# Layer 1 of an expert layer by lookup: 768 columns of V read densely instead of gathered

## What the reference computes

```python
for i in range(DEPTH):                       # DEPTH = 2, 256 tokens, D_MODEL = 2048
    h = rms_norm(x, norm_mix_g[i])
    y = mla_mixer(h, ...) if i % 2 == 0 else fox_mixer(h, ...)
    x = x + y
    h = rms_norm(x, norm_ffn_g[i])
    x = x + peer_ffn(h, peer_w_q[i], peer_sub_keys[i], peer_u[i], peer_v[i])

def peer_ffn(h, w_q, sub_keys, u, v):        # 8 heads, 128 keys a side, 16384 experts, top 16
    q = (x @ w_q).reshape(t, PEER_HEADS, 2, PEER_D_HALF)
    scores = jnp.einsum('thcd,cnd->thcn', q, sub_keys)
    top_s, top_i = lax.top_k(scores, PEER_TOPK)
    cand_s = top_s[..., 0, :, None] + top_s[..., 1, None, :]
    cand_i = top_i[..., 0, :, None] * PEER_N_KEYS + top_i[..., 1, None, :]
    best_s, pos = lax.top_k(cand_s.reshape(...), PEER_TOPK)
    idx = jnp.take_along_axis(cand_i.reshape(...), pos, axis=-1)
    g = jax.nn.softmax(best_s, axis=-1)
    # for each block of 128 tokens, n_sel = 8 heads x 16 = 128 experts a token
    u_sel = u[i_blk]
    a = gelu(einsum('tkd,td->tk', u_sel, x_blk), approximate=False) * g_blk
    return einsum('tk,tkd->td', a, v[i_blk])
```

## Time and profile before

| what | us |
|---|---|
| median of 3 runs | 3615.15 (3604.41 to 3617.04) |
| the profiled execution | 3612.59 |
| its span in the profile | 3610.6 |
| TensorE busy | 2886.4 |
| VectorE busy | 2035.0 |
| GpSimd busy | 1465.2 |
| ScalarE busy | 945.4 |
| data moved by DMA | 1345.35 MB |

### The profile page before, as it was taken

One profiled execution on the slowest core, in us unless ns is written; L12 is line 12 of the kernel. 1 busy time (PEld: TensorE's weight loads), 2 busy tenths in 40 slices (PEclk: granted clock), 3 DMA queues, 4 the chain that ended last, 5 costly groups with the idle time before them and its releaser, 6 DMA issues.

```text
span 3610.6 us, 26702 instructions
## 1 busy us (share of the span) xinstructions
PE 2886.4 (80%) x7322; PEld 1357.2 (38%) x7322; DVE 2035.0 (56%) x3584; ACT 945.4 (26%) x2349; POOL 1465.2 (41%) x1065
## 2 busy tenths in 40 slices
PE   7888977777777888888888788998988777777776
PEld 6445743333332433333333343443433322222222
DVE  2333166666667554555464655455546466677765
ACT  3334322222222222323221222232322122222221
POOL 4002545555565322222342532222244355555554
PEclk8877989899998999999998899999999898888888
DMA  4212589999999999999999999999999999999998
GB/s 147 79 61 89 177 358 416 416 416 416 415 410 422 418 417 418 417 417 414 412 396 399 418 418 417 417 417 417 413 411 399 399 371 421 421 422 421 421 419 351
DMA packets 262853, 1345.35 MB, mean 373 GB/s; under 512 B 27200, under 2 KB 48192, under 8 KB 130368
## 3 DMA queue, kind: packets, MB, share of 16 engines
q0 software_dynamic: 147456, 1073.81, 72.0%
q1 hardware_dynamic: 115264, 269.99, 19.9%
HBM read 1341.62 MB, written 2.10 MB: 372 GB/s over the span
## 4 chain that ended last, share of the span: by engine, by line
DMA 60%; PE 20%; issue 12%; POOL 3%; DVE 3%; ACT 1%; SPq 1%; DVEq 0%; POOLq 0%; ACTq 0%
DMA room<-in_peer_v_dram,index 50%; PE psum L977 11%; DMA wbuf<-in_fox_w_o_dram 5%; PE psum L1026 3%; DMA wbuf<-in_peer_w_q_dram 3%; DMA room<-in_peer_u_dram,index 2%; POOL room L668 1%; PE psum L1041 1%; PE psum L740 1%; PE psum L741 1%; PE psum L742 1%; POOL room L678 1%; DVE resid L1974 0%; SPq L536 0%; POOL w_low L652 0%
## 5 line engine op out<-in xcount | busy, mean ns | idle before, releaser
L977 PE MATMUL psum<-room,diag 128*128 128x512 f32 x3072 | 1612.9, 667 | 565.4 <-DMA room<-in_peer_v_dram,index 517.6
L1963 DVE CUSTOM_DVE_ANT_0 room<-room,normed 128x2048 f32<-128x2048 f32 x512 | 1172.7, 2290 | 619.7 <-DMA room<-in_peer_u_dram,index 615.8
L678 POOL DMA_INDIRECT room<-in_peer_v_dram,index x512 | 757.3, 1479 | 1096.8 <-PE psum L977 1040.4
L977 PEld LDWEIGHTS psum<-room,diag 128*128 128x128 f32 x3072 | 605.2, 208 | 1510.5 <-issue 1257.7
L668 POOL DMA_INDIRECT room<-in_peer_u_dram,index x512 | 591.6, 1155 | 719.2 <-DVE dots L1963 468.7
L1392 ACT ACTIVATE acts<-dots 128x1 f32<-128x1 f32 x512 | 103.4, 202 | 1779.6 <-DVE dots L1963 1779.1
L1974 DVE SCALAR_TENSOR_TENSOR resid<-room,acts,resid 128x512 f32<-128x512 f32 x512 | 384.6, 751 | 308.1 <-DMA room<-in_peer_v_dram,index 239.7
L1041 PE MATMUL psum<-wbuf,normedT 128*128 128x512 f32 x1024 | 464.0, 596 | 0.0
L1026 PE MATMUL psum<-wbuf,normedT 128*128 128x512 f32 x512 | 273.5, 684 | 78.5 <-DMA wbuf<-in_fox_w_o_dram 40.7
L1041 PEld LDWEIGHTS psum<-wbuf,normedT 128*128 128x128 f32 x1024 | 189.2, 190 | 215.5 <-issue 212.9
L652 POOL TENSOR_TENSOR w_low<-wbuf,w_high 128x2048 fp32r<-128x2048 f32 (+1 forms) x28 | 114.0, 4081 | 306.0 <-ACT w_high L1247 306.0
(11 more groups left out here) (199 smaller groups left out, 1794.2 us busy)
## 6 DMA issues: line engine op xcount, KB each, us to landing
wbuf<-in_fox_w_in_dram SPq DMA_DIRECT2D x128, 1024.0 KB, 12.6
wbuf<-in_fox_w_o_dram SPq DMA_DIRECT2D x32, 1024.0 KB, 31.8
wbuf<-in_peer_w_q_dram SPq DMA_DIRECT2D x32, 1024.0 KB, 28.1
wbuf<-in_mla_w_o_dram SPq DMA_DIRECT2D x16, 1024.0 KB, 5.2
wbuf<-in_peer_w_q_dram SPq DMA_DIRECT2D x32, 512.0 KB, 20.1
wbuf<-in_mla_w_in_dram SPq DMA_DIRECT2D x8, 1024.0 KB, 8.2
wbuf<-in_mla_w_kvb_dram SPq DMA_DIRECT2D x32, 256.0 KB, 3.4
room<-in_peer_u_dram,index POOLq DMA_INDIRECT x512, 17.0
```

The source lines that it names most:

```text
L678: pool.indirect_dma_start(v_ring[:, r, :], None, v_table, bass.IndirectOffsetOnAxis(index[:, number % 2, s:s + 1], 0)).then_inc(v_full[r], 16)
L977: mm = pe.matmul(psum[:, q, :], diag[:, r, :], v_ring[:, r, q * TILE:(q + 1) * TILE], start=at == 0, stop=at == WINDOW - 1, skip_group_che ...
L1963: V.tensor_tensor_reduce(u_ring[:, r, :], u_ring[:, r, :], normed[:, b, :], 1.0, 0.0, ALU.mult, ALU.add, dots[:, r:r + 1]).then_inc(dot_do ...
```

## The change

Layers and windows 0 and 1 stay as they are. In layer 1 the 256 full V gathers go away, and so do `accumulate` and `axpy` for windows 2 and 3. Columns 768 to 2047 are still gathered (`gather_part`, rows of 5 KB). Of these 256 gathers, 88 are issued in window 3 and summed by TensorE with diagonal matrices that ScalarE builds; the other 168 come after the last dot and are added by VectorE, one operation each (`add_part`). GpSimd issues them all, on the queue of the U gathers.

Columns 0 to 767 are not gathered. SP reads all 16384 rows of V's layer 1 once, as 128 tiles of 128 rows with 3 KB of each row, into four buffers (`load_dense`). The rows of tile i are the experts whose first key is i; its partitions are the second key. TensorE multiplies each tile with a matrix of second key by token, for each of the two token blocks, and sums all 128 tiles in PSUM (`dense`). These spread matrices have to be built first. The keys and the weights of a block are transposed, so that slots lie on partitions; for each token, VectorE builds a one-hot of the second key and a one-hot of the first key times the weight (`one_hots`, four tokens a call: one comparison over 128x512 and four operations over 128x128), TensorE multiplies the two (`spread_tokens`), and ScalarE copies the product into the spread matrix with a stride of 128 elements (`copy_spread`). Block 0 has its 32 calls in window 3; block 1 has its 32 calls after the last dot. The spread matrix of block 0 takes the place of the weight buffer, that of block 1 the whole of `room`, where the U ring was.

```diff
+DENSE = 768
+KEPT = D - DENSE
+GATHERED = 2 * WINDOW
+SPLIT = 2 * WINDOW
+LAST = 3 * WINDOW
+ON_PE = 88
+TOKENS = 4
+BUILDS = P // TOKENS
+BUILD_AT = 8
+def v_at(m):
+    return 3 + m * 124 // ON_PE
+def build_at(g):
+    return BUILD_AT + g * 7 // 2
...
+        spread = [a.rearrange("p (i t) -> p i t", i=KEYS) for a in (wbuf[:, :, :, :].rearrange("p h k n -> p (h k n)"),
+                                                                   room[:, :])]
...
+        v_part = [old_T[:, r * KEPT:(r + 1) * KEPT] for r in range(3)] + [scores_ahead[:, 0:KEPT]]
+        v_tile = [normed[:, 1, 0:DENSE], normed[:, 1, DENSE:2 * DENSE], scores[:, 0:DENSE], scores[:, DENSE:2 * DENSE]]
...
+            def load_dense(i):
+                r = i % RING
+                if i == 0:
+                    sp.wait_ge(dot_done, UNITS * SLOTS)
+                    sp.wait_ge(index_ready, UNITS)
+                if i >= RING:
+                    sp.wait_ge(tile_used, i - RING + 1)
+                sp.dma_start(v_tile[r], peer_v[1][i * KEYS:(i + 1) * KEYS, 0:DENSE]).then_inc(tile_full[r], 16)
...
+            def gather_part(m):
+                b, at, r = m // WINDOW, m % WINDOW, m % RING
+                if m == 0:
+                    pool.wait_ge(late_ready, 1)
+                    pool.wait_ge(score_done, 8)
+                if at % SLOTS == 0 and b:
+                    pool.wait_ge(index_ready, 3 * PHEADS + at // SLOTS + 1)
+                if RING <= m < ON_PE + RING:
+                    pool.wait_ge(part_summed, m - RING + 1)
+                if m >= ON_PE + RING:
+                    pool.wait_ge(part_added, m - RING - ON_PE + 1)
+                pool.indirect_dma_start(v_part[r], None, v_table,
+                                        bass.IndirectOffsetOnAxis(late_place[b][:, at:at + 1], 0),
+                                        element_offset=DENSE).then_inc(part_full[r], 16)
...
-                gather_v(n)
+                if n < SPLIT:
+                    gather_v(n)
...
+                for m in range(ON_PE):
+                    if n == LAST + v_at(m):
+                        gather_part(m)
...
+            for m in range(ON_PE, GATHERED):
+                gather_part(m)
...
+            def sum_part(m):
+                r = m % RING
+                if m == 0:
+                    pe.wait_ge(peer_added, 2)
+                pe.wait_ge(diag2_ready, m + 1)
+                pe.wait_ge(part_full[r], 16 * (m // RING + 1))
+                for c0 in range(0, KEPT, TILE):
+                    n = min(TILE, KEPT - c0)
+                    mm = pe.matmul(psum[:, c0 // TILE, 0:n], diag[:, r, :], v_part[r][:, c0:c0 + n],
+                                   start=m == 0, stop=m == ON_PE - 1, skip_group_check=True)
+                mm.then_inc(part_summed, 1)
...
+            def spread_tokens(b, g):
+                number = BUILDS * b + g
+                bank = 6 + g % 2
+                pe.wait_ge(hot_ready, number + 1)
+                if number > 1:
+                    pe.wait_ge(spread_done, number - 1)
+                for t in range(TOKENS):
+                    last = pe.matmul(psum[:, bank, t * P:(t + 1) * P], hot_key[g % 2][:, t, :], hot_act[g % 2][:, t, :],
+                                     start=True, stop=True)
+                last.then_inc(spread_full, 1)
+            def dense(i):
+                r = i % RING
+                pe.wait_ge(tile_full[r], 16 * (i // RING + 1))
+                if i == 0:
+                    pe.wait_ge(spread_done, NB * BUILDS)
+                    pe.wait_ge(sums_closed, 1)
+                for b in range(NB):
+                    for c0, n, bank in ((0, TILE, 3 + 2 * b), (TILE, DENSE - TILE, 4 - 2 * b)):
+                        mm = pe.matmul(psum[:, bank, 0:n], spread[b][:, i, :], v_tile[r][:, c0:c0 + n],
+                                       start=i == 0, stop=i == KEYS - 1, skip_group_check=True)
+                mm.then_inc(tile_used, 1)
...
-                    accumulate(n)
+                    if window < 2:
+                        accumulate(n)
+                    if window == 3:
+                        last_window(at)
...
+                for at in range(WINDOW, WINDOW + 4):
+                    last_window(at)
+                turn_tables(1)
+                for g in range(BUILDS):
+                    spread_tokens(1, g)
+                for i in range(KEYS):
+                    dense(i)
...
+                    nc.scalar.activation(act_of[n // WINDOW - 2][:, at:at + 1], acts[:, 0, r:r + 1], ACT.Copy,
+                                         scale=gates[:, number % 2, s:s + 1]).then_inc(diag_ready, 1)
+                    return
...
+            def copy_spread(b, g):
+                act.wait_ge(spread_full, BUILDS * b + g + 1)
+                dst = spread[b][:, :, TOKENS * g:TOKENS * (g + 1)].rearrange("p i t -> p t i")
+                nc.scalar.activation(dst, psum[:, 6 + g % 2, :].rearrange("p (t i) -> p t i", t=TOKENS),
+                                     ACT.Copy).then_inc(spread_done, 1)
...
+            def one_hots(b, g):
+                number = BUILDS * b + g
+                if g == 0:
+                    dve.wait_ge(turned_done, b + 1)
+                    dve.wait_ge(iota_ready, 2)
+                if number > 1:
+                    dve.wait_ge(spread_full, number - 1)
+                tokens = slice(TOKENS * g, TOKENS * (g + 1))
+                step(V.tensor_tensor(hot_key[g % 2], iota_key[1].unsqueeze(1).broadcast_to([P, TOKENS, KEYS]),
+                                     turned[b][:, 1, tokens].unsqueeze(2).broadcast_to([P, TOKENS, KEYS]), ALU.is_equal))
+                for t in range(TOKENS):
+                    at = TOKENS * g + t
+                    last = V.tensor_scalar(hot_act[g % 2][:, t, :], iota_key[0], turned[b][:, 0, at:at + 1],
+                                           turned[b][:, 2, at:at + 1], ALU.is_equal, ALU.mult)
+                    if t < TOKENS - 1:
+                        step(last)
+                chain.settle()
+                last.then_inc(hot_ready, 1)
...
+            def add_part(m):
+                b, at, r = m // WINDOW, m % WINDOW, m % RING
+                dve.wait_ge(part_full[r], 16 * (m // RING + 1))
+                dve.wait_ge(part_added, m - ON_PE)
+                if b and at == 0:
+                    dve.wait_ge(diag_ready, UNITS * SLOTS)
+                cols = resid[:, b, DENSE:D]
+                V.scalar_tensor_tensor(out=cols, in0=v_part[r], scalar=late_act[b][:, at:at + 1], in1=cols,
+                                       op0=ALU.mult, op1=ALU.add).then_inc(part_added, 1)
...
-                    if n:
+                    if 0 < n <= SPLIT:
                         axpy(n - 1)
-                    if at == 0 and n:
+                    if n in (WINDOW, SPLIT):
...
+                close_parts()
+                for g in range(BUILDS):
+                    one_hots(1, g)
+                    if g % 2:
+                        add_part(ON_PE + g // 2)
+                for m in range(ON_PE + BUILDS // 2, GATHERED):
+                    add_part(m)
+                for b in range(NB):
+                    add_dense(b)
```

151 lines of the change are left out of this document (139 added, 12 removed).

## The result

| | before | after |
|---|---|---|
| median | 3613.76 us (8 runs, 3604.41 to 3617.04) | 3628.01 us (8 runs, 3624.61 to 3639.84) |
| ratio | | 1.0046 [1.0037, 1.0055] |
| profiled execution, its span | 3612.59, 3610.6 us | 3628.41, 3626.7 us |

The changed kernel is 0.46% slower. The difference is real (the interval leaves out 1), but lies inside the 0.5% that the forecast called no change. The forecast was 3600 us, some 15 us less than before; measured were 14 us more. It was 28 us too low: 3628.01 us lies 3 us above its own range of 3578 to 3625, though inside the wider 3545 to 3650.

What follows compares the result with a forecast made beforehand. DMA traffic was taken to bound the kernel. The stages summed as 2062 + 606 + 466 + 8 + 75 + 369 + 8 = 3594 us of span, given as 3600 us; own range 3578 to 3625, over all cases 3545 to 3650.

Steps and rivals of the forecast that it cites:

- What is removed: Layer 1's V traffic: 637 us of gathers become 530 us of part gathers and dense tiles, at most 107 us less.
- bridge: Between the last dot's window and block 1's builds: last activation, sum, transposes, copy and closing addition, about 8 us.
- Window 2: Layer 1, block 0, with block 1's attention beside it: from 898 to 606 us, bounds 579 and 650.
- slower rival: Layer 1, block 0: attention handshakes set the pace, 645 us there and 3639 us in all; decides from 640; chance 0.24.
- Window 3: Layer 1, block 1: from 644 to 466 us, 458 of transfers plus 8 lost; bounds 458 and 490.
- The signs named for this stage: Layer 1, block 1, in the profile after: about 3.6 us a slot at over 410 GB/s.
- Builds: Block 1's 32 spread-matrix calls after the last dot: 75 us, VectorE at 1.5 us a call plus 16 part additions.
- the full-gain rival: Whole layer 1: all gained but for the builds (1.25 us a call, 66 us); 3553 us; chance 0.28.
- Dense phase: 128 dense tiles and remaining parts at the end: DMA longest at 356 us, 369 us in all, bounds 350 and 395.
- the 2.8 named as a sign: Dense tiles at the end, in the profile after: 128 tiles about 2.8 us apart, TensorE over 90% busy.
- The clock rival: Dense tiles at the end: TensorE granted clock 0.84, its 328 us become 390, time about 3634 us; chance 0.10.

Runs made afterwards that it cites:

- half_dots_w3: Changed kernel with dots over 1024 of 2048 columns in window 3, all gathers whole: 3600.89 us; window 3 took 464.8 us.
- narrow_parts: Changed kernel with every part gather moving 256 of its 1280 columns, number, order and waits kept: 3569.08 us; window 3 took 483.3 us.
- experiment 8: Changed kernel with 32 instead of 16 parts taken in block 1's builds, every other one summed by TensorE: 3594.86 us against 3612.87 before, ratio 0.9947.
- tiles4: Changed kernel with 4 instead of 128 dense tiles: 3581.89 us; the 152 parts took 331 us, 2.18 us each.
- five_buffers: Changed kernel with a fifth buffer for part gathers once the builds are done: 3625.8 us in one run; 1.92 us a part after the last tile.

## Why the prediction was wrong

Point by point, by its own steps:

- **What is removed: right.** 1.58 us a part lies within 1.48 and 1.64 measured alone, and half_dots_w3 had window 3 with its bridge in 465 us at 417 GB/s, so the 458 us of transfers in it were there to be had.
- **Window 2: right in its sum**, 604 for 606, less so in its terms. VectorE has 395 us of work in it, as worked out, the dots are 5.2 us apart in the input projection, and they wait 40 us for U, not 137. But 15 of the added us were given to the waits of the attention, and the DMA share is 1.01 through all its heads: those waits did not leave the DMA idle. It moved 402 and 391 GB/s at that share, not 417, and its idle time lies in the last 60 us, where the forecast put 5 and 7 us. So some of the agreement is luck. No run tested the division. The slower rival (640 and more) is out.
- **Window 3: the step that failed, with 20 us.** "U has four buffers and loses only the time that the DMA has nothing else: 8 us". The forecast had the order of GpSimd's issues in view but put no price on an issue. One is held while a dot runs: 1.82 us for a U gather, 1.35 for a part, against 0.94 alone. 125 issues of the one kind are 228 us and 88 of the other 119; with 0.3 us between all, 411 us of 494 for GpSimd, beside 400 us of work on VectorE and a DMA share of 0.97. Each waits for the others in rings of four buffers, and the forecast took the largest of the three loads (458 us of transfers) for the stage's time. Taking away bytes (narrow_parts) gave 10 us and one_hots 6; halving the dots gave 29, and leaving the part gathers out 70, of which 59 are the issues and waits without the bytes. How the 20 us divide between the hold and the coupling with VectorE stays open. The signs named for this stage came out wrong with it: 3.8 us a slot for 3.6, and 389 GB/s for over 410.
- **A price was in the trace of before**, in GpSimd's groups of window 3, which the forecast didn't read:

```profile
L678 POOL DMA_INDIRECT room<-in_peer_v_dram,index x125 | 198.8, 1590 | 214.6 <-PE psum L977 192.7 <-DVE resid L1974 18.3 <-issue 3.7
L668 POOL DMA_INDIRECT room<-in_peer_u_dram,index x123 | 142.1, 1155 | 73.4 <-DVE resid L1974 43.5 <-issue 15.5 <-DVE dots L1963 14.4
```

Two issues took 2.75 us and 0.6 between them of a slot of 4.98 us; GpSimd had 288 us of idle time. By the same durations a slot of the new window 3, with a part gather in 88 of 128, would need 2.8 us of 3.6 (an estimate). It needed 3.2 of 3.8, since the U issue rose from 1.16 to 1.82 us: the old rows give a warning, not the whole price.
- **Builds: right**, 78 for 75. A one_hots call took 1.63 us, not 1.5: its four small operations are 344 ns each, above both ends taken for them (0.13 and 0.285), and overlap to 1.11 us. The faster call of the full-gain rival (1.25) is out too. ScalarE's strided copy took 1.04 to 1.06 us, not 0.6, hidden as said. An addition took 1.55, as said. The DMA moved 159 GB/s; experiment 8, with 16 more parts in this stage, came out 33 us below the kernel after by the medians.
- **Dense phase: the second failure, 15 us.** "The DMA is the longest ... whichever stream ends first leaves the other its own pace, so 369 us." TensorE's 2.56 us a tile and 328 us were nearly right (332 measured, at clock 1.00). But it was TensorE that set the pace: the tiles came 2.6 us apart, not the 2.8 named as a sign. Beside it the DMA share was full too, and a part came every 2.6 us (128 in 332 us). 23 were left; by the forecast's own 1.58 and 0.98 it would have been about 17. Their own pace is 2.2 us, not the transfer's 1.58: the forecast gave the time behind TensorE's 328 us 41 us, and it took 50 from the last tile to the last part, with the DMA at 0.83. That pace is the loop through four buffers in part, by tiles4 (2.18) and five_buffers (1.92); the issues held by the additions lengthen it.
- **Rivals.** The full gain asked for 3553; its window 2 and window 3 did not come. The clock rival is out: 1.00 was granted in the whole dense phase. That the streams of the tail leave each other a remainder was named, and priced too low.

So the changed kernel saves the bytes that it was said to save, and gives all of it back. Against the forecast's own pure transfer times, window 2 loses 25 us (604 for 579), window 3 with its bridge 36 (494 for 458), the builds 49 (80 us at 159 GB/s instead of 417), and what follows them 28 (384 for 356). The first and third were foreseen; 20 and 15 us in the others were not. The two misses have the same sign, so nothing cancelled them.

## What to carry to other kernels

When transfers shrink, put the issuing engine in the account with the durations that its instructions have beside the work of that stage, not with the shortest one. Here engines of 400 and 411 us of work beside 458 us of transfers took 494 us with the bridge, each waiting for the others through four buffers; to take the largest of the three is a lower bound. Look in the trace of before for issues that last longer beside the work of another engine. For a stream at the end of a kernel, take the round trip through its buffers (2.2 us an item here) and not its transfer (1.6), and look for a stage with idle DMA before it (0.52 in the builds) that can take some of its items.
